# A greedy list order for the first half of a hybrid encoder layer, and one weight chunk split into idle buffers

## The reference

```
u = rms_norm(x) @ W_in                       # 1024 -> 2560: q, k, v (512 each), conv a and gate (512 each)
a = neighbourhood_attention(q, k, v, rpb)    # 8 heads of 64, window of rows x 16 columns, relative bias
c = silu(layer_norm(conv31(conv_a * sigmoid(gate))))   # depthwise, 31 taps, 512 channels
x = x + concat(rms_norm(a), rms_norm(c)) @ W_out
x = x + hier_moe(rms_norm(x))                # 32 experts 1024 -> 512 -> 1024, two per token
y = rms_norm(x)
```

## Time and profile before

| what | us |
|---|---|
| median of three runs (lowest, highest) | 1010.12 (1006.12, 1015.42) |
| profiled execution, whole time | 1011.13 |
| its span in the trace | 1009.1 |
| PE busy | 865.1 (86%) |
| DVE busy | 412.6 (41%) |
| ACT busy | 244.1 (24%) |
| PE's granted clock, mean | 0.924 of 2.4 GHz |

### The profile page before, as it was taken

The page is one execution under the profiler, slowest core; times in us unless marked ns, Lnnn a source line. Parts: engine busy times, 40 slices in busy tenths (PEclk is TensorE's granted clock), DMA queues, the critical chain, the costliest instruction groups (busy, mean ns, idle before and its releaser), DMA issues.

```text
span 1009.1 us, 15368 instructions
## 1 busy us (share of the span) xinstructions
PE 865.1 (86%) x5812; PEld 598.4 (59%) x5813; DVE 412.6 (41%) x613; ACT 244.1 (24%) x484; POOL 103.1 (10%) x181
## 2 busy tenths in 40 slices
PE   3988889999789999299999987988799999799920
PEld 2888768777478889155555554544455556455500
DVE  6498767698834432622222211211121222122236
ACT  5222272825543223011111110101111111011111
POOL 4100001000001010010000000000000000000045
PEclk9999899999967979589999999999999999999965
DMA  7433634331060733959999999999999999999155
GB/s 195 116 81 77 192 116 156 117 95 42 2 208 1 300 158 108 376 207 396 397 398 400 396 407 403 412 413 406 403 411 399 395 393 390 416 397 387 50 190 194
DMA packets 80489, 267.39 MB, mean 265 GB/s; under 512 B 17289, under 2 KB 43145, under 8 KB 55881
## 3 DMA queue, kind: packets, MB, share of 16 engines
q1 hardware_dynamic: 60640, 235.66, 61.3%
q0 software_dynamic: 6880, 19.41, 5.6%
q10 hardware_dynamic: 12936, 11.88, 3.6%
HBM read 248.05 MB, written 24.99 MB: 271 GB/s over the span
## 4 chain that ended last, share of the span: by engine, by line
PE 56%; SPq 18%; DMA 10%; DVE 6%; ACT 3%; issue 3%; POOL 2%; POOLq 0%; ACTq 0%; DVEq 0%
SPq L721 18%; PE ps L1148 13%; PE ps L946 12%; DMA ring<-in_w_up 9%; PE ps L1073 7%; PE ps L1181 7%; PE ps L942 4%; PE ps L1151 2%; PE ps L1139 2%; POOL ring L901 1%; PE ps L1160 1%; PE ps L1016 1%; PE ps L965 1%; PE ps L635 1%; PE ps L995 1%
## 5 line engine op out<-in xcount | busy, mean ns | idle before, releaser
L1151 PE MATMUL ps<-ring,big 128*64 128x256 f32 x896 | 209.1, 392 | 23.8 <-DMA ring<-in_w_up 23.8
L1148 PE MATMUL ps<-ring,big 128*64 128x256 f32 x896 | 211.0, 392 | 3.6 <-DMA ring<-in_w_gate 2.2
L1148 PEld LDWEIGHTS ps<-ring,big 128*64 128x64 f32 x896 | 125.0, 141 | 65.1 <-issue 18.4
L1151 PEld LDWEIGHTS ps<-ring,big 128*64 128x64 f32 x896 | 125.5, 142 | 51.4 <-DMA ring<-in_w_up 30.1
L946 PE MATMUL ps<-hT,w_split 128*128 128x512 f32 (+1 forms) x768 | 145.7, 349 | 8.1 <-DVE hT L1462 3.6
L1740 DVE TENSOR_TENSOR big<-ps,big 64x256 f32<-64x256 f32 x78 | 33.2, 426 | 277.7 <-ACT big L1404 277.7
L946 PEld LDWEIGHTS ps<-hT,w_split 128*128 128x128 f32 x768 | 122.0, 196 | 25.6 <-issue 6.5
L1506 DVE SCALAR_TENSOR_TENSOR big<-big,vec 128x783 f32<-128x783 f32 x116 | 119.7, 1032 | 3.1
L1404 ACT ACTIVATE big<-ps 64x256 f32<-64x256 f32 x78 | 29.3, 376 | 313.5 <-PE ps L1151 313.5
L1182 PE MATMUL ps<-ring,big 128*64 128x512 f32 x224 | 102.1, 598 | 0.0
L1181 PE MATMUL ps<-ring,big 128*64 128x512 f32 x224 | 102.1, 598 | 0.0
(11 more groups left out here) (195 smaller groups left out, 1076.2 us busy)
## 6 DMA issues: line engine op xcount, KB each, us to landing
ring<-in_w_gate SPq DMA_DIRECT2D x44, 1024.0 KB, 28.6
ring<-in_w_up SPq DMA_DIRECT2D x44, 1024.0 KB, 29.5
ring<-in_w_down SPq DMA_DIRECT2D x44, 1024.0 KB, 30.1
big<-in_w_gate SPq DMA_DIRECT2D x20, 1024.0 KB, 29.5
big<-in_w_up SPq DMA_DIRECT2D x20, 1024.0 KB, 30.0
big<-in_w_down SPq DMA_DIRECT2D x20, 1024.0 KB, 29.7
w_raw<-in_w_in SPq DMA_DIRECT2D x20, 512.0 KB, 4.1
rows<-big ACTq DMA_DIRECT2D x39, 256.0 KB, 6.5
```

The costliest lines, as they stand in the source:

```text
L1148: pe.matmul(ps[0:BLK, 6 * h, 0:FH], xT[:, k, :], gate_w[s][:, k, fs], start=(k == 0), stop=(k == KD - 1))
L1151: mm = pe.matmul(ps[BLK:2 * BLK, 6 * h + 1, 0:FH], xT[:, k, :], up_w[s][:, k, fs], start=(k == 0), stop=(k == KD - 1))
```

## The change

The list is now made by a list scheduler. `parts()` names every piece of work with its cost and its predecessors; pieces of one kind stay in line. `plan()` keeps a time per engine (PE, DVE, ACT, POOL, and the transfers of SP as one engine "DMA") and takes again and again, on the engine that can start first, the ready piece with the lowest number in `FIRST` (ready within 0.1 us, on DVE within 0.25 us). Scores, turns, values and the spreading of sums are separate pieces with lower numbers than `win` and `po` (the output group). ACT's strips, squares, copies and splits are pieces as well, and a change of ACT's table is charged 1.3 us. The last twelve output groups, the second norm, the transposes and the logits are ordered in the same way.

`CHUNKS` has qk 2 and conv 3 exchanged: now (..., qk 1, qk 2, conv 3, qk 3). The two runs of v 1 are split into a new buffer `w_early`, which lies over the attention result and one of the first norm's buffers, both idle then; the runs after it reuse the `w_split` buffers of v 0 (`run_before`). SP loads run 0 before the last two tiles of x.

```diff
-CHUNKS = [("conv", 0), ("conv", 1), ("v", 0), ("v", 1), ("qk", 0), ("conv", 2), ("qk", 1), ("conv", 3), ("qk", 2), ("qk", 3)]
+CHUNKS = [("conv", 0), ("conv", 1), ("v", 0), ("v", 1), ("qk", 0), ("conv", 2), ("qk", 1), ("qk", 2), ("conv", 3), ("qk", 3)]
+EARLY_RUNS = tuple(2 * CHUNKS.index(("v", 1)) + sub for sub in range(2))
...
+COST = dict(part=1.42, narrow=1.47, ht=0.9, sc=0.65, tn=0.45, va=0.6, inv=1.42, mean=1.28, var=0.75, rows=1.5, ssc=2.9, asum=0.75,
+            po=2.85, tnh=1.7, lgt=0.9,
+            lo=1.24, tap=1.04, first=0.7, last=1.75, bias=1.5, sh=1.05, rinv=0.2, norm=1.05, alo=1.03, wlo=2.3, xc=0.97, rstd=0.2,
+            zn=0.97, clo=1.02, sscc=0.2, ssac=0.2, px=0.78, h2=1.29,
+            hi=1.07, strip=0.84, ex=2.05, tc=0.62, vo=0.95, ahi=0.92, asq=0.84, sqx=0.84, silu=1.03, chi=0.95, csq=0.84, whi=1.95,
+            sq2=1.27, tch=1.05, rootl=1.6, roota=1.6, rootc=1.6, root2=0.9, load=4.7, rawl=5.0, wload=6.5, raws=0.1)
...
+FIRST = dict(win=50, ht=1, sc=10, tn=8, va=8, inv=7, mean=15, var=2, rows=0, ssc=3, asum=6, po=45, tnh=20, lgt=2,
+             glu=0, lo=1, tap=60, bias=20, sh=5, rinv=4, norm=4, alo=12, wlo=15, xc=9, rstd=0, zn=9, clo=9, sscc=0, ssac=2, px=1, h2=0,
+             out=0, hi=1, strip=40, ex=5, tc=3, vo=2, ahi=12, asq=14, sqx=9, silu=9, chi=9, csq=6, whi=15, sq2=0, tch=0,
+             rootl=0, roota=0, rootc=0, root2=0, load=0, rawl=1, wload=2, raws=0)
+TABLE = dict(ex="exp", silu="silu")
+HANDOVER, LANDING, PATIENCE, SWITCH = 0.13, 2.0, dict(DVE=0.25), 1.3
...
+    for k in range(ASLOTS):
+        j, t = divmod(k, NT)
+        in_line(("sc", k), ([("out", CHUNKS.index(("qk", j)), 3)] if t == 0 else []) + ([("sh", k - 1)] if k else []))
+        in_line(("sh", k), [("sc", k)] + ([("bias", 2 * j + 1)] if t == 0 else []) + ([("ex", k - 1)] if k else []))
+        in_line(("ex", k), [("sh", k)] + ([("tn", k - 2)] if k >= 2 else []))
+        in_line(("tn", k), [("ex", k)] + ([("tc", k - 1)] if k else []))
+        in_line(("tc", k), [("tn", k)] + ([("va", k - 1)] if k else []))
+        in_line(("va", k), [("tc", k)] + ([("out", CHUNKS.index(("v", 1)), NT - 1)] if k == 0 else [])
+                + ([("vo", j - 1)] if j and t == 0 else []) + ([("norm", j - 1)] if j and t == 4 else []))
+    for j in range(PAIRS):
+        in_line(("rinv", j), [("ex", NT * j + NT - 1)])
+        in_line(("vo", j), [("va", NT * j + NT - 1)])
+        in_line(("inv", j), [("rinv", j), ("vo", j)])
+        in_line(("norm", j), [("inv", j)])
+        in_line(("ahi", j), [("norm", j), last_group])
+        in_line(("alo", j), [("ahi", j)])
+        in_line(("asq", j), [("norm", j), ("sh", ASLOTS - 1)] + ([("asum", j - 3)] if j >= 3 else []))
+        in_line(("asum", j), [("asq", j), ("tc", ASLOTS - 1)])
...
+def run_before(run):
+    if run in EARLY_RUNS or run < 2:
+        return None
+    return run - 4 if run - 2 in EARLY_RUNS else run - 2
...
+    while len(order) < len(work):
+        now, engine = min((max(free[e], min(waiting.values())), e) for e, waiting in ready.items() if waiting)
+        soon = now + PATIENCE.get(engine, 0.1)
+        name = min((n for n, at in ready[engine].items() if at <= soon),
+                   key=lambda n: (FIRST[n[0]], ready[engine][n], number[n]))
+        now = max(now, ready[engine].pop(name))
+        cost = work[name][0]
+        needs = "sigmoid" if name[0] == "out" and CHUNKS[name[1]][0] == "conv" else TABLE.get(name[0])
+        if needs and needs != table:
+            cost, table = cost + SWITCH, needs
+        free[engine] = over[name] = now + cost
+        order.append(name)
...
+        with ExitStack() as middle:
+            middle.enter_context(nc.sbuf_tensor("under_big", [P, MID], F32))
+            w_early = middle.enter_context(nc.sbuf_tensor("w_early", [P, 2, 2, KD, P], F32R))[:]
...
-            load_win(0)
+                elif t == NTS - 1:
+                    load_win(0)
...
+                if run in EARLY_RUNS:
+                    act.wait_ge(win_done, 1)
+                elif run >= 2:
+                    act.wait_ge(win_done, run_freed(run_before(run)))
+                nc.scalar.activation(split_of(run)[:, run % 2, 0], w_raw[:, run % 2], ACT.Copy).then_inc(hi_done, 1)
```

More of the change, by code:

```diff
@@ new lines, in taker, with last_part, release @@
+def taker(c, g):
+    return ("glu" if CHUNKS[c][0] == "conv" and g >= 2 else "out", c, g)
+def run_before(run):
+    if run in EARLY_RUNS or run < 2:
+        return None
+    return run - 4 if run - 2 in EARLY_RUNS else run - 2
+def last_part(run):
+    c, sub = divmod(run, 2)
+    return ("win", c, NT - 1, 1) if CHUNKS[c][0] == "v" else ("win", c, 2 * sub + 1, 1)
+def plan():
+    work = parts()
+    number = {name: n for n, name in enumerate(work)}
+    missing = {name: len(after) for name, (_, after) in work.items()}
+    followers = {}
+    for name, (_, after) in work.items():
+        for d in after:
+            followers.setdefault(d, []).append(name)
+    ready, free, over, order, table = {e: {} for e in ENGINES}, dict.fromkeys(ENGINES, 0.0), {}, [], None
+    def release(name):
+        engine, at = ENGINE[name[0]], 5.0 if name[0] == "strip" else 0.0
+        for d in work[name][1]:
+            other = ENGINE[d[0]]
+            at = max(at, over[d] + (LANDING if other == "DMA" else 0.0) + (HANDOVER if other != engine else 0.0))
+        ready[engine][name] = at
+    for name in work:
+        if not missing[name]:
+            release(name)
+    while len(order) < len(work):
[10 more added lines that the diff above has]
+        order.append(name)
+        for other in followers.get(name, ()):
+            missing[other] -= 1
+            if not missing[other]:
+                release(other)
@@ L669, in _ @@
             for what, *a in ORDER:
-                if what == "lo" and a[0] + 2 < RUNS:
-                    load_win(a[0] + 2)
+                if what == "load" and a[0] >= 4:
+                    load_win(*a)
                 elif what == "raws":
@@ L1116, in _ @@
                     sum_squares()
-                elif what == "out":
+                elif what == "po":
                     out(*a)
-                elif what == "turn":
+                elif what == "tnh":
                     turn_h2(*a)
-            logits(pe, NT - 1)
+                elif what == "lgt":
+                    logits(pe, *a)
             pe.wait_ge(both_ready, 1)
```

426 lines of the change are left out of this document (155 added, 271 removed).

## The result

The changed kernel takes 1000.35 us (median of 4 runs, 999.71 to 1001.04) where the kernel before took 1010.35 (median of 4, 1006.12 to 1015.42): a ratio of 0.9899, with a 95% interval of 0.9853 to 0.9945. The forecast was 982 us, a gain of 28. The direction holds, the size does not. That the time lies inside the range of 967 to 1003 is luck: the upper end was put there for rival 1, the clock among the products, and this is not what filled it. The profiled execution of the changed kernel took 1001.04 us, its span is 998.8.

What follows compares the result with a forecast made beforehand. Bound by PE up to the router, then by the weight stream and PE in turns. 10.9 + 4.5 + 1.7 - 3 + 21.7 - 8 = 27.8 off 1011.1 gives 983.3, median 982; range 967 to 1003.

Steps and rivals of the forecast that it cites:

- rival 1: Output products: sums among them hold PE at half clock, groups take 4.67 instead of 2.77, +21, time 1003; chance 0.10.
- Early split of v 1: Projection chunks v 1 and qk 0: both waits and the clock they cost go, a gain of 10.9 us.
- new stalls: Waits that the new list itself brings, engines being in order: a loss of 3 us, bounds 0 and 10.
- Attention inside conv 2: PE's wait before scores in conv 2 and the half clock behind it: gain 4.5 us, bounds 6.4 and 0.
- wait before qk 2: PE's wait at 207.52 us behind a `glu` goes, since glu gets first place on DVE: gain 1.7 us.
- rival 3: Slower: PE stands before eagerly placed pieces in 18 slots inside the projection, 45 us lost, 1028; chance 0.08.
- From the last projection to the first output product: The tail between these two points shrinks from 56.2 to 34.5 us: gain 21.7, bounds 14 and 27.
- Output products: Last attention sum, last mean and four variances move in among the output products: loss 8 us, bounds 5 and 13.
- The rule on the clock: "A busy PE is a fast PE" would make tail sums 1.3 each, 3 to 4 us less; prediction kept 2.6.
- Rival 2: Taps of conv block 3 end 12 us later than 275, the conv half's products wait 8: 990; chance 0.10.
- Rival 4: The weight stream sets the end by its bytes alone, and the time stays at 1010; chance 0.03.

Runs made afterwards that it cites:

- Patience: The changed kernel with 1.0 us instead of 0.25 us for which DVE may wait for an urgent piece rather than start a tap: 997.39 us, ratio 0.9879.
- 80 columns: The changed kernel with attention's sums of squares and the variances made with 80 result columns instead of one, same number of matmuls: 1000.8 us, ratio 0.9909.

## Why the prediction was wrong

*Early split of v 1: right as a mechanism; 10.9 forecast, 8.2 measured.* v 1 starts right behind v 0 (85.14) and qk 0 behind v 1 (102.19), both waits gone, at full clock: v 1 takes 17.20 us. But the prediction held v 0's wait at 2.5 and its length at 17.54, and the new list made them 4.05 and 18.82. DVE's timeline of the changed kernel has a part of the reason:

```profile
63.50 0.61 DVE L1465 TENSOR_TENSOR big<-ps,big 128x256 f32<-128x256 f32 x1
64.14 1.04 DVE L1485 SCALAR_TENSOR_TENSOR big<-big,vec 128x783 f32<-128x783 f32 x1
65.21 1.23 DVE L1446 TENSOR_TENSOR w_split<-w_raw,w_split 128x1024 fp32r<-128x1024 f32 x1
```

A tap of 1.04 us, which nobody awaits, stands ahead of the low part for which PE waits, and the `glu` before it starts half a microsecond later than before, behind two taps. Patience took 0.96 of the wait away and left the length. The 1.3 of length are clock (0.91 from 64 to 84 us, against 1.00 before); why it fell is not shown. Together these are 2.8 us, about the 3 that the prediction held for "new stalls". The split is worth 8.2 on the new list and 5.4 on the old.

*Attention inside conv 2, wait before qk 2, rival 3: right.* From the start of qk 0 at 102 us to 243 PE has no gap (76.00 busy of 76 from 102 to 178, 65.00 of 65 from 178), at full clock, and none of the slots inside the projection made PE wait, so rival 3's stalls did not come. Part of this gain is not in the milestone of 243.1, since the list also did three values, two turns and one spreading more inside the projection than the order before, some 4.1 us of PE's work. With them the first half gained 14.4 us, against 14.1 forecast: the 3.8 that are missing at the last projection are this moved work. The prediction did not see it, and its 28.8 for the tail, a chain of steps each of which waits for the one before, could not get shorter by it.

*From the last projection to the first output product: the step that failed.* Forecast were 34.5 us, measured 50.9, outside the bound of 42 that the prediction gave for "all sums in the path". The six slots are 3.0 us apart (243.85 to 258.86), against 3.2 forecast. The sums are what failed. It began with the reading of the kernel before: the earlier trace rows and the words on its order have the four attention sums ahead of the product, but the four variances stood there too, as its timeline of PE shows:

```profile
286.81 1.47 PE L1038 MATMUL ps<-ones,big 128*128 128x1 f32 x12 [2.56 <-DVE big L1555]
...
288.80 2.37 PE L1038 MATMUL ps<-ones,big 128*128 128x1 f32 x12
...
293.85 2.72 PE L1038 MATMUL ps<-ones,big 128*128 128x1 f32 x12
...
307.00 2.70 PE L1038 MATMUL ps<-ones,big 128*128 128x1 f32 x12
```

With the 10.40 of attention that makes 19.7 us of sums ahead of the product before the change, and 21.0 after it. The sums stayed where they were.

The prediction exposed two of the three attention sums, at 2.6 each: all three are (7.81), ahead of the last values, and the last mean then ran at half clock (3.1) too. It put the fourth attention sum and the four variances among the products, at 1.3 each: they stand ahead of the first one. So 11.7 us were charged for eight sums that took 21.0. By the times that `plan()` computes, `var` 0 and `var` 1 are placed before the product is ready, and `FIRST`, where `var` has 2 and `asum` 6 against 45 of `po`, lets `asum` 3, `var` 2 and `var` 3 pass it too. In the plan, at 0.75 us each, the product starts 2.7 us after it is ready; on the chip, at half clock, 12.0. The prediction read the list's numbers for `asum` against `va`, and not for `var` and `asum` against `po` in the same place.

*Output products: a second step that failed, hidden in the total.* Forecast were 102 us from first product to last logits; it is 100.0, against 95.1 before. No attention sum or variance lies in it, so the 8 us that I charged there were paid ahead of it, and "from there to the last logits nothing else changes: 94 us" was wrong by 6. It is not the clock among the products: over the first 58 us from the first product that is 0.91, against 0.88 before. It is the last tile, which the new list leaves until the end:

```profile
387.25 1.97 PE L1065 MATMUL ps<-ident,big 128*128 128x128 f32 x8 [2.55 <-DVE big L1570]
390.33 3.63 PE L611 MATMUL ps<-wr,big 128*128 128x36 f32 x16 [1.11 <-ACT big L1332]
```

Waits of 2.55 and 1.11 us, and behind them 5.6 us of work that the kernel before did in 2.9 (1.07 and 1.87 for the same counts), come to 6.3, of which the conv half's sums gave 1.8 back (5.80 instead of 7.58). Every kernel with the new list waits twice at this place, the two with the old list (the kernel before and the early split alone) do not.

*The rule on the clock.* By the Trainium skill ("TensorE: Matmul & The Clock Gate", "What's actually happening") activity releases the throttle; here PE was busy for 12.80 of 13 us at 0.50 just before the product, and 13.00 of 13 with 80 columns. The trace does not agree with that, if it is read as "a busy PE is a fast PE". Keeping 2.6 against 1.3 was right where the prediction kept it. It then used 1.3 for the five pieces among the products, on the argument that the clock is full there, and the experiment with the sums behind the products shows that this argument is half true: 24 of these sums' rows in the trace do take 2.7 to 3.8 us there, instead of 5.25, and the products beside them are slow (4.2 and 5.5 us a group instead of 2.8).

*Rival 2, DVE last:* the taps of block 3 ended at 267.5, earlier than the 275 of the prediction, and no product of the conv half waited. *Rival 4, not passed on:* refuted. In all the profiled executions the span ends 602 to 606 us after the last logits, also where these end 33 us earlier than before.

The missing 18.2 us up to the last logits, by milestones: 3.8 in the projection, 16.4 in front of the first product, 2.0 back in the products. By the prediction's terms: 3.8 in the projection, 9.3 for the eight sums (21.0 against 11.7), 1.5 for the last mean (3.1 against 1.6), 6.1 for the products without sums (100.0 against 93.9), less 2.5 for the rest of the tail (26.8 against 29.3).

What stays open: why the same wait of 2.54 us before v 0 left the clock full in the kernel before (17.54 us for 144 matmuls) and not in the one with the early split alone (19.01); why the clock stays at half through busy stretches of narrow sums; by how much patience helps by itself, as 3.0 us is within the intervals; and what another order of the last tile would be worth, which no run tried.

## What to carry over

Look for the one place where the critical operand is being made: read from both lists, the old and the new, which pieces stand ahead of it there, and price them at the clock that the trace shows, not at full clock. A gain from moving work exists only if the work stood in the way before and does not after. Before moving many small reductions around, make them fewer: moved, they cost 13.4 us where they went and slowed or held up the products there by another 10.6 (in all 6.5 us slower); added up first on an engine with room, they were worth 16 us. Then look at the end of a stage as well as at its start: the last tile alone cost some 6 us here. And compare the parts of a change by themselves: here the split alone gave 5.4 of the 10 us, and the list alone none that can be told.

## What the hardware showed

One row of the trace for a float32 matmul with one result column (two rows for each matmul of the program) cost 217 ns at clock 0.50 (2.6 us for twelve) and about 122 at full clock (1.47 for twelve), and with 80 columns 224 ns at 0.50, while PEld was busy for 13.00 of 13 us: within these widths its time does not follow the result's width. PE's being busy did not bring the clock back (12.80 of 13 us at 0.50). After the same wait of 2.54 us the clock once stayed full (144 matmuls in 17.54 us) and once fell (19.01).
